# Running the two token tiles of a layer stack one after the other, with the first tile's gathered rows beside the second tile's layers

## The reference, cut to what matters

```
x = x + gt2 * (square(relu(h @ ffn_w1)) @ ffn_w2)      # h = modulated rms_norm(x); 4096 wide
x = rms_norm(x, final_g)                                # end of the first block
h = rms_norm(x, norm_mix_g_2)
p = h @ w_in_2                # q, k, v of two attentions, 8 forget columns, 2 x 1024 gate columns
a = causal attention, 8 heads, rotary;   b = causal attention, 8 heads, with forget terms
x = x + (gate_a * (a @ w_branch_a) + gate_b * (b @ w_branch_b)) @ w_out_2
h = rms_norm(x, norm_ffn_g_2)
q = h @ w_peer_q_2            # 8 heads, two half keys of 128 each
for each token and head: 16 best of 128 for either half, then 16 best of their 256 sums
    x += sum over the 16 of softmax weight * gelu(h . u[row]) * v[row]
out = rms_norm(x, norm_final_g_2)
```

## Time and profile before

| | us |
|---|---|
| median of three runs | 1623.27 |
| the profiled run | 1619.43 |
| its span, first to last instruction | 1618.1 |
| TensorE busy | 1289.6 (80%) |
| VectorE busy | 926.0 (57%) |
| ScalarE busy | 298.4 (18%) |
| GpSimd busy | 394.1 (24%) |
| DMA | 414.99 MB, 256 GB/s over the span |

### The profile page before, as it was taken

The page is one execution under the profiler, slowest core; times in us unless marked ns, Lnnn a source line. Parts: engine busy times, 40 slices in busy tenths (PEclk is TensorE's granted clock), DMA queues, the critical chain, the costliest instruction groups (busy, mean ns, idle before and its releaser), DMA issues.

```text
span 1618.1 us, 12477 instructions
## 1 busy us (share of the span) xinstructions
PE 1289.6 (80%) x4248; PEld 750.7 (46%) x4248; DVE 926.0 (57%) x2091; ACT 298.4 (18%) x703; POOL 394.1 (24%) x317
## 2 busy tenths in 40 slices
PE   2989999979999998999999690576666766666666
PEld 2875655645766756675544680222222222222222
DVE  6288868563011003222232439998888888888764
ACT  2242111212000002123131111111111121111111
POOL 0001212110110000200000116566444444455440
PEclk9999999979999999999999895798888888888888
DMA  9624443544353443432223538999999999999993
GB/s 369 234 112 154 149 159 115 204 156 169 142 197 141 196 156 128 160 129 106 103 104 128 240 127 348 421 421 422 421 421 421 422 422 421 422 421 421 422 422 134
DMA packets 50752, 414.99 MB, mean 256 GB/s; under 512 B 5888, under 2 KB 8192, under 8 KB 8960
## 3 DMA queue, kind: packets, MB, share of 16 engines
q0 software_dynamic: 36864, 268.45, 40.0%
q1 hardware_dynamic: 12672, 142.15, 23.1%
q10 hardware_dynamic: 1152, 3.59, 0.6%
HBM read 413.11 MB, written 1.05 MB: 256 GB/s over the span
## 4 chain that ended last, share of the span: by engine, by line
PE 48%; DMA 24%; DVE 22%; issue 3%; ACT 2%; another core or an unknown queue 0%; ACTq 0%; DVEq 0%; SPq 0%
PE ps L333 31%; DMA arena<-in_euv,arena 15%; DMA ring<-in_euv,arena 8%; PE ps L713 6%; PE ps L417 5%; DVE xr L1761 4%; DVE arena L1734 4%; PE ps L803 3%; DVE ring L1734 2%; DVE arena L1029 1%; DVE arena L1296 1%; DVE arena L1303 1%; PE ps L978 1%; DMA ring<-in_ada 0%; DMA ring<-in_glu 0%
## 5 line engine op out<-in xcount | busy, mean ns | idle before, releaser
L978 PE MATMUL ps<-arena 128*128 128x512 f32 x420 | 240.0, 722 | 100.8 <-ACT arena L2199 100.8
L333 PE MATMUL ps<-hT,ring 128*128 128x256 f32 (+1 forms) x1488 | 294.5, 359 | 23.3 <-DVE hT L1060 10.2
L2306 POOL DMA_INDIRECT arena<-in_euv,arena x151 | 189.3, 1253 | 444.7 <-DVE arena L1726 247.3
L333 PEld LDWEIGHTS ps<-hT,ring 128*128 128x128 f32 x1488 | 258.5, 196 | 58.6 <-DVE hT L1060 10.4
L978 PE MATMUL ps<-ring,arena 128*128 128x512 f32 x224 | 131.8, 734 | 114.1 <-ACT arena L2199 114.1
L1734 DVE CUSTOM_DVE_ANT_0 arena<-arena 128x1024 f32<-128x1024 f32 x151 | 181.4, 1221 | 50.1 <-DMA arena<-in_euv,arena 49.9
L978 PEld LDWEIGHTS ps<-arena 128*128 128x128 f32 x420 | 94.2, 231 | 243.3 <-ACT arena L2199 129.2
L978 PEld LDWEIGHTS ps<-ring,arena 128*128 128x128 f32 x224 | 50.5, 233 | 189.4 <-ACT arena L2199 129.2
L333 PE MATMUL ps<-arena 128*128 128x128 f32 (+4 forms) x732 | 122.5, 313 | 13.0 <-ACT arena L1820 7.1
L2306 POOL DMA_INDIRECT ring<-in_euv,arena x79 | 103.0, 1304 | 115.3 <-PE ps L978 39.2
L333 PEld LDWEIGHTS ps<-arena 128*128 128x128 f32 (+1 forms) x732 | 102.3, 194 | 49.1 <-issue 34.6
(11 more groups left out here) (297 smaller groups left out, 1317.2 us busy)
## 6 DMA issues: line engine op xcount, KB each, us to landing
ring<-in_w SPq DMA_DIRECT2D x16, 2048.0 KB, 8.0
ring<-in_ada SPq DMA_DIRECT2D x12, 2048.0 KB, 8.0
ring<-in_gates SPq DMA_DIRECT2D x8, 2048.0 KB, 7.9
ring<-in_qkv SPq DMA_DIRECT2D x6, 2048.0 KB, 7.9
ring<-in_wp SPq DMA_DIRECT2D x5, 2048.0 KB, 8.3
ring<-in_g SPq DMA_DIRECT2D x4, 2048.0 KB, 7.8
ring<-in_pq SPq DMA_DIRECT2D x4, 2048.0 KB, 8.2
ring<-in_o_ab SPq DMA_DIRECT2D x2, 2048.0 KB, 8.4
```

Of the source, the lines that this page charges most:

```text
L333: ins = te.matmul(o, l, r, start=(i == 0), stop=(i == len(pairs) - 1))
L978: ins = te.matmul(ps[b][:], diag[:, added % 8, :], slots[slot_of[n]][:, D + hf * 512:D + (hf + 1) * 512], start=(b not in opened), stop=(e ...
L2306: gp.indirect_dma_start(slots[i], None, A["euv"], bass.IndirectOffsetOnAxis(ap=idx[:, tt, e:e + 1].bitcast(U32), axis=0)).then_inc(gathere ...
```

## The change

From `w1` on, the layers are written as a list of units for one token tile (`late_units`), and every engine goes through `late_units(0)` first and then `late_units(1)` (`last_order`). The weights are in `STREAM` twice. Up to the end of tile 0 the ring has three slots; for tile 1 it has two, and the third holds expert rows. Among the units of tile 1 stand `AMONG` = 52 groups of two rows each, spaced by the units' costs; the other 76 groups follow. Each engine keeps that order: in `group(g)` VectorE takes a piece of a `choose` in every second group, the first dot, the shares of the group before, then the second dot.

With it: all column products run on 128 columns in one PSUM bank. VectorE squares instead of GpSimd. The forget terms enter the scores as a product of 8 rows with a broadcast column of the identity, not one of 128 rows with `lbt`. `qT_`, `fT`, `yT`, `qp` and `sg2` are half or less of their size, so 8 slots hold rows at first, and 16 from row 114 on, once tile 1's last scores are taken. `rowb`, `rowb2` and `keys` are loaded once for each tile, at other places in SyncE's list. The first gathers wait for `pq` 2 of tile 0. The rows on VectorE are every fourth from the start.

```diff
+def late_units(tt):
+    ups = [(("up", j), 7) for j in range(8)]
+    downs = [(("down", j), 7) for j in range(8)]
+    yield ("fT",), 1
+    yield ups[0]
+    for j in range(8):
+        if j < 7:
+            yield ups[j + 1]
+        yield downs[j]
...
+    yield ("x1",), 1
...
+    yield from (gate(0, 1), gate(1, 0), gate(1, 1), (("branch", 0, 0), 2), pt(1, 0), (("branch", 0, 1), 2), pt(1, 1),
...
+                gate(3, 1), (("branch", 1, 0), 2), (("branch", 1, 1), 2), (("yT",), 1), (("wout", 0), 7),
+                (("wout", 1), 7), (("e",), 1), (("pq", 0), 9), (("choose", 0), 0), (("pq", 1), 9), (("choose", 1), 0),
+                (("pq", 2), 9), (("pq", 3), 9))
...
+SECOND = PLACE[("w1", 0, 1)]
+SPOT = [n % RING if n < SECOND else (n - SECOND) % 2 for n in range(len(STREAM))]
...
-GROUP = 4
+GROUP = 2
...
+AMONG = 52
+
+
+def last_order():
+
+    for u, _ in late_units(0):
+        if u != ("fT",):
+            yield u, 0
+    units = list(late_units(1))
+    total, cost, g = sum(c for _, c in units), 0, 0
+    for u, c in units:
+        yield u, 1
+        cost += c
+        while g < AMONG and g * total < cost * AMONG:
+            yield ("group", g), None
+            g += 1
...
-            def split_gemm(w, tt, names):
...
+            def columns(name, key, tt, chunks):
+
+                w = weights(*key)
+                if chunks[0] == 0:
+                    te.wait_ge(*loaded(*key))
+                    take(name, "main")
+                for c in chunks:
+                    ins = mm(psum(name)[:, c * 128:(c + 1) * 128],
+                             [(w[:, k * 512 + c * 128:k * 512 + c * 128 + 128], hT[:, k, tt * 128:(tt + 1) * 128])
+                              for k in range(8)])
...
+            fresh = [2, 2]
+            for u, tt in last_order():
+                if u[0] == "group":
+                    if u[1]:
+                        add_rows(u[1] - 1)
...
+                elif what == "up":
+                    o = f4(fT[:, i % 2, :, :])
+                    v.wait_ge(*empty(f"up{tt}.{i}"))
+                    tell(v.tensor_tensor(o, o, o, ALU.mult), "squared")
...
+            def group(g):
+                step, k = g // PER_STEP, g % PER_STEP
+                if k % 2 == 0 and step + 2 < len(STEPS) and step + 2 not in (8, 9):
+                    if k == 0:
+                        pieces[0] = choose(step + 2)
+                    next(pieces[0], None)
+                dot_row(GROUP * g)
+                if g:
+                    add_rows(g - 1)
+                for n in range(GROUP * g + 1, GROUP * g + GROUP):
+                    dot_row(n)
...
+            def group(g):
+                step, n = g // PER_STEP, GROUP * g
                 if g:
                     diagonals(g - 1)
...
+                sc.wait_ge(sig("dotted"), g + 1)
...
                 elif i < n_early:
-                    gp.wait_ge(*empty("yT1.1"))
+                    gp.wait_ge(*full("sc0.0"))
+                    gp.wait_ge(*spent[STREAM[[m for m in range(SECOND) if SPOT[m] == 2][-1]]])
...
+                    if key == ("w1", 1, tt):
+                        sy.wait_ge(sig("x_added"), 4)
+                        if tt:
+                            sy.wait_ge(sig("xn"), NORMED["e0"])
+                        sy.dma_start(gt[:, 0, :], A["rowb"].broadcast_to([P, D])).then_inc(sig("l_fg"), 16)
```

More of the change, by code:

```diff
@@ L688, in tensor @@
             out_rows("w_o", 1, 0, "wo")
-            te.wait_ge(sig("xn"), 1)
-            rows_T(xn, 0, "fT0")
+            te.wait_ge(sig("xn"), NORMED["f0"])
+            rows_T(xn[:, 0, :], "fT0")
             out_rows("w_o", 1, 1, "wo")
[L694 to L702, removed]
@@ L852, in branch_out @@
-            def branch_out(kind, tt, hf):
-                key, name = ("bb" if kind else "ba", 0), f"bo{kind}.{tt}{hf}"
-                if tt == 0 and hf == 0:
-                    te.wait_ge(*loaded(*key))
-                    te.wait_ge(*empty(f"pv{kind}1.3"))
-                w, o = weights(*key), take(name, "main")
-                mm(o[:], [(yT[:, 4 * kind + c, tt * 128:(tt + 1) * 128],
-                           w[:, c * D + hf * 512:c * D + hf * 512 + 512]) for c in range(4)]).then_inc(*fill(name))
-                spent[key] = full(name)
@@ L895, in tensor @@
-            for i in (2, 3):
-                for tt in range(2):
-                    for part in range(2):
-                        gate2(i, tt, part)
-                        next(gen_1, None)
-                        next(gen_1, None)
-            for _ in gen_1:
-                pass
-            branch_out(1, 0, 0)
-            branch_out(1, 0, 1)
-            branch_out(1, 1, 0)
-            te.wait_ge(sig("merged2"), 2)
-            rows_T(merged, 0, "yT0")
-            branch_out(1, 1, 1)
@@ L964, in tensor @@
[L964 to L983 removed]
+                    spent[key] = full(name)
@@ new lines, in add_rows @@
+            def add_rows(g):
+                for n in range(GROUP * g, GROUP * g + GROUP):
+                    if on_vector(n):
+                        continue
+                    tt, e = PICKS[n]
+                    added[0] += 1
+                    te.wait_ge(sig("diag"), added[0])
+                    for hf in range(2):
+                        name = f"sum{tt}.{hf}"
+                        if name not in held:
+                            hold(name, 4 + 2 * tt + hf)
+                        ins = te.matmul(psum(name)[:], diag[:, added[0] % 8, :],
+                                        slots[slot_of[n]][:, D + hf * 512:D + (hf + 1) * 512],
+                                        start=(fresh[tt] > 0), stop=(e == 127))
+                        fresh[tt] -= 1
+                    ins.then_inc(sig("row_added"), 1)
+                    slot_done[n] = (sig("row_added"), added[0])
@@ L1773, in last_own @@
                 return own, n_own[0]
-            for _ in choose(0):
-                pass
-            rows_T(1, "eT1")
-            for _ in choose(1):
-                pass
-            groups = len(PICKS) // GROUP
-            for g in range(groups):
-                step = g // PER_STEP
-                if g % PER_STEP == 0 and step + 2 < len(STEPS):
-                    pieces = choose(step + 2)
-                next(pieces, None)
-                dot_rows(g)
-                if g:
-                    add_rows(g - 1)
-                if g == groups // 2 + 2:
-                    finish(0)
-            add_rows(groups - 1)
-            finish(1)
+            pieces = [iter(())]
+            for u, tt in last_order():
+                if u[0] == "group":
+                    group(u[1])
+                elif u[0] == "end":
+                    add_rows(GROUPS - 1)
+                elif u[0] == "finish":
+                    finish(tt)
+                else:
+                    late(tt, *u)
         def scalar():
```

1048 lines of the change are left out of this document (434 added, 614 removed).

## The result

The changed kernel takes 1683.23 us (median of 4 runs, 1682.17 to 1684.74) against 1623.41 for the kernel before beside it. The ratio is 1.037, with an interval from 1.035 to 1.039: slower by 60 us. The forecast was 1657, 34 above the kernel before, with a range from 1575 to 1725. The span of the profiled run is 1682.7 us.

What follows compares the result with a forecast made beforehand. TensorE was taken to bound the layers, memory the expert rows. First tile to 694.5 us, second tile with 104 rows from 705.5 to 1272, remaining gathers to 1638, tail 15: span 1653, forecast 1657 us, range 1575 to 1725.

Steps and rivals of the forecast that it cites:

- Stage 1: First token tile alone through the layers, from 395.1 us to the end of its `pq` units at 694.5 us.
- Stage 2: Second tile's layers with 104 rows brought in among them: 566 us, from 705.5 to 1272 us.
- The stalls: Second tile's layers: TensorE's waits, mostly before diagonals, 45 us among the pairs and 59 later, 104 us together.
- The ring of two: Two weight slots during the second tile: 10 us taken; nothing if loads take 8 us, 100 if 20.
- 20 for the clock: Second tile's layers: lower granted clock costs 5% of 408 us of TensorE work, 20 us; ends 0 and 100.
- the price of an added row: TensorE's adds: four passes of 0.43 us, 1.72 us a row, 134 us for 78 rows among the second tile's layers.
- Rival B: Second tile's layers: pauses hold the clock down, 50 to 80 us more, 1720 us; granted clock under 0.9; chance 0.12.
- Stage 3 and tail: After the layers: 144 gathers at 2.54 us take 366 us, to 1638; then 15 us of tail, span 1653.
- A (the stalls overlap): Second tile's layers: the 104 us of stalls shrink, likely 1575 us; decided by under 530 us there; chance 0.27.
- C (the ring of two): Second tile's weight loads take 20 us, +90, 1745 us; TensorE would wait for `ring`; chance 0.05.
- D (rows that don't come in): Late adds hold the eight slots, DMA share near 0.5 beside the second tile's layers; 1656 us; chance 0.06.
- check from the other side: Second tile without rows about 300 us plus 104 rows 264, together 564 against 566: the overlap gives back nothing.

Runs made afterwards that it cites:

- filled: Changed kernel with TensorE's pauses before the diagonals filled by matmuls with zero weights, 72 us of idle work: 1666.52 us, ratio 1.027.
- mended: Changed kernel with adds one group later, forget product padded to 128 rows, softmax weights of the first choices later, tile 0's `rowb` load one weight tile later: 1571.02 us.
- the later addition: Changed kernel with TensorE adding each group's rows one group later: 1583.16 us, ratio 0.975 to the changed kernel.
- run 1583: Not a run number but a time in us: the changed kernel with rows added one group later, measured 1583.16 us.
- the small tiles: Changed kernel loading only 64 columns of each weight tile in the second pass, all waits and row gathers kept: 1682.14 us, ratio 1.037.
- the run apart: Changed kernel with no expert rows among the second tile's layers, all 52 groups coming after them: 1691.78 us, ratio 1.042.
- run 17: Not a run number but 17 us saved: the changed kernel with zero-weight matmuls in TensorE's pauses, measured 1666.52 us.

## Why the prediction came out as it did

The sign was right; a loss of 34 us was forecast and one of 60 measured. Compared with its own sum of 1653, the profiled span is 29.7 us longer. (From span to time 5.1 us were added, which gives 1658 and not 1657; here the two differ by 0.5, so the forecast is off by 26.) It comes from four places.

**Stage 1: 11 us.** The eight pairs ended at 519.2 (516.0 forecast; 1.3 us of that is a later start), the wait for the `w1` tile was 3.74 us (4), the seam at x1 ended at 529.9 (526.0), the seam at the last norm at 667.5 (658.5), and the `pq` units at 714.3 (694.5). TensorE's timeline of the changed kernel:

```profile
526.64 1.97 PE L419 MATMUL ps<-K,arena 128*128 128x128 f32 x8 [7.40 <-DVE arena L1468]
529.88 10.10 PE L403 MATMUL ps<-hT,ring 128*128 128x128 f32 x64 [1.28 <-DVE hT L1032]
...
667.49 9.59 PE L403 MATMUL ps<-hT,ring 128*128 128x128 f32 x64 [0.72 <-issue]
...
702.30 2.05 PE L403 MATMUL ps<-arena 128*128 128x128 f32 x8 [6.33 <-ACT arena L1742]
704.14 8.32 PE L403 MATMUL ps<-hT,ring 128*128 128x128 f32 x64
```

The seams had about their durations in the sum, but not the slow products behind them: 64 matmuls cost 10.10 and 9.59 us instead of 7.31 (2.8 and 2.3 more), the scores with 8 rows about 2 and the gate behind them 2. The unexplained pause at 702 costs 7.5 (6.33 instead of 0.77 idle, and two slow groups), the start and the pairs 3.2, the two seams 2; some other steps were put 2 or 3 too high. A product of 8 rows was put at the price of one with 128, by its passes; the clock made it dearer. Nearly half of these 20 us did not reach stage 2. The weight tile was issued at 701.56 and landed after 11.3 us, between the row's 12.6 and the 10.5 that the prediction estimated from the rule of the Trainium skill (DMA: Bandwidth & Descriptors, Queues, rings and completion order). But TensorE was held by its queries until 714.3, so the load that was to be exposed for 11 us was covered. Tile 2 starts at 716.86, 11.4 later than forecast.

**Stage 2: the total right to 6 us, by errors that cancel.** It ends at 1289.6, after 573 us instead of 566. The stalls were counted well: 34.2 us in 9 places up to 926 (45 forecast) and 59.7 in 25 places after (59), together 94 against 104. The ring of two cost 0, not 10, and the seams some 6 less. The mis-sized term is the clock: 408 us of work and 20 for the clock were put, and TensorE was busy for 466.5. The filled and the mended kernels give back 39 and 41 of the 58 above 408 (425.5 from 707 to 1180 us, a window with the same work); what is left, 17 to 19, stands at a clock of 0.95 to 0.96 and was not taken apart. Some 50 of the 58 lie in the additions, the first work behind each pause. TensorE's groups in the layers of the second tile, first the changed kernel (714 to 1293 us), then the mended one (707 to 1185):

```profile
L934 PE MATMUL ps<-arena 128*128 128x512 f32 x208 | 124.9, 744 | 65.7 <-ACT arena L2050 65.7
...
L806 PE MATMUL ps<-ring,arena 128*128 128x512 f32 x128 | 57.7, 604 | 0.0
L934 PE MATMUL ps<-ring,arena 128*128 128x512 f32 x98 | 57.5, 740 | 28.2 <-ACT arena L2050 28.2
```

```profile
L934 PE MATMUL ps<-arena 128*128 128x512 f32 x212 | 97.4, 594 | 1.4 <-ACT arena L2056 1.4
...
L934 PE MATMUL ps<-ring,arena 128*128 128x512 f32 x104 | 53.1, 658 | 10.6 <-ACT arena L2056 10.6
```

That is 182.4 us for 306 passes, 0.60 each, against 150.5 for 316, 0.48 each: 37 us at equal count, while `down` took the same in both within 2 us. The step that failed is the price of an added row, 1.72 us, worked out from passes without a pause (`down`'s 13.73 us for 32, and the 24 at the end), with too small a term for the clock beside it. The rows added behind waits in the last stage of the kernel before were there to be read; its groups from 974 to 1600 us:

```profile
L978 PE MATMUL ps<-arena 128*128 128x512 f32 x402 | 232.3, 728 | 100.8 <-ACT arena L2199 100.8
L978 PE MATMUL ps<-ring,arena 128*128 128x512 f32 x220 | 129.9, 737 | 114.1 <-ACT arena L2199 114.1
```

362.2 us for 622 passes are 0.58 each, 2.33 a row: with 78 rows 48 us more than at 1.72, where 20 had been put. Rival B did look at those windows, but set the 12.9 us of 30 passes against the 17.25 of the row with 36, where 16.56 belong; its "up to a third" is close to the 35% of the whole stage by luck. The Trainium skill (TensorE: Matmul & The Clock Gate, HAM oscillation — how this bites in real kernels) describes that pattern, bursts between waits that start again at half clock, and this trace agrees: four passes in 3.78 us at 727.77.

**Stage 3 and tail: 10 and 2 us.** The layers moved 310 GB/s x 579 us = 179 MB where 183 were put, so some 4 rows more were left, about 9 us. The last landing is at 1666.1, the tail 16.6 instead of 15.

**The rivals.** A (the stalls overlap) did not happen: they were waited for in full, and stage 2 was far over 530. But its time was within reach of the later addition: with most of the stalls gone, stage 2 takes 470 (462 with all mends) and the run 1583 (1571), near the 1575 named for its likely form. B (the clock) is half true: its mark, a granted clock under 0.9, came with 0.89, at a price of 40 to 58 us instead of the forecast's 20; the run stayed well under its 1720. The sign "`w1` passes of 0.114 us throughout" failed with it: 64 took up to 10.10 us. By the prediction's own marks, both B's and the end of stage 1 more than 15 us from 694 came out against it. C (the ring of two) is excluded by the waits and by the small tiles. D (rows that don't come in) is excluded by the window from 714 to 926 us, a DMA share of 0.89. The "check from the other side", that the overlap gives back nothing, is nearly confirmed by the run apart, 8.5 us, though both of its sides were too low: the second tile alone took 324 us and not 300, with the rows 573 and not 566.

## What to carry to other kernels

When a second stream of work is interleaved with the first in one fixed order on every engine, look for the shortest chain from one engine's unit to the next one's need, and give it a unit of slack. Here one group of delay was worth 100 us, and turned a loss of 60 into a gain of 40. Price a recurring pause of TensorE as the pause plus what the products behind it lose, 1 to 3 us each here (40 to 58 us for 34 pauses), and multiply it by the number of pauses. Before transfers are hidden under an engine's work, ask what the engine's added work costs there: 104 rows took 142 us of the layers' time to save 250 in the mended kernel, and 248 to save 257 with the waits in place.

## What the runs showed of the hardware that was not expected

- With products whose operand has 8 rows (between ones of 64), the granted clock fell toward the lower level, 1.2 GHz, while TensorE was busy without a pause: 0.67 over 15 us, against 1.00 with the same product padded with zeros to 128 rows. Two products took 0.79 us in place of 0.48.
- 72 us of multiplications by zero in the pauses made the run 17 us shorter (clock from 0.89 to 0.95), and 130 us less of additions between pauses made TensorE busy for only 85 less (0.84).
- With the first eight gathers on their way, ScalarE stood still for 4.2 us, and TensorE behind it for 6.3, for no cause that the profile shows.
